# The xo projection and the MLP in one block, weights split by halves of K in a ring of five

## The reference, cut to what matters

```python
    o = jnp.einsum("bhsm,bmhd->bshd", probs, v).reshape(bsz, s, D_MODEL)
    return o @ w_xo                                   # 1024 x 1024, added to x
...
        x = x + memory_cross_attention(rms_norm(x, norm_xattn[i]), mem_n, w_q[i], w_kv[i], w_xo[i])
        hm = rms_norm(x, norm_mlp[i])                 # y = x * rsqrt(mean(x*x) + 1e-6) * gain
        x = x + jnp.square(jax.nn.relu(hm @ w_up[i])) @ w_down[i]     # 1024 -> 4096 -> 1024
    return rms_norm(x, norm_final)
```

## Time and profile before

| | us |
|---|---|
| median of 3 runs | 3066.21 (3064.24 to 3067.56) |
| span of the profiled execution | 3067.1 |
| PE busy in it | 2940.0 (96%) |
| DVE, POOL, ACT busy | 1510.3, 1127.4, 769.7 |
| mean granted clock of PE | 0.987 of full |

### The profile page before, as it was taken

One profiled execution on the slowest core, in us unless ns is written; L12 is line 12 of the kernel. 1 busy time (PEld: TensorE's weight loads), 2 busy tenths in 40 slices (PEclk: granted clock), 3 DMA queues, 4 the chain that ended last, 5 costly groups with the idle time before them and its releaser, 6 DMA issues. The chain is left out here.

```text
span 3067.1 us, 48431 instructions
## 1 busy us (share of the span) xinstructions
PE 2940.0 (96%) x20270; PEld 2330.9 (76%) x20270; DVE 1510.3 (49%) x1510; ACT 769.7 (25%) x1106; POOL 1127.4 (37%) x632
## 2 busy tenths in 40 slices
PE   7999888999999999999999999999999799989999
PEld 6776777778878767788888888777887677866677
DVE  6454443233375343741615235677678433357561
ACT  5433232320011032100100001324233332357410
POOL 1331223444344412444444444411221453435552
PEclk8999999999999999999999999999999999999999
DMA  6243332442141101111111111122233534321143
GB/s 213 75 134 114 96 93 78 139 121 69 40 139 55 55 28 42 48 48 42 50 45 48 48 48 48 42 62 83 84 102 95 164 106 126 114 86 63 57 139 124
DMA packets 324919, 258.05 MB, mean 84 GB/s; under 512 B 46754, under 2 KB 285529, under 8 KB 324746
## 3 DMA queue, kind: packets, MB, share of 16 engines
q1 hardware_dynamic: 324490, 255.47, 27.7%
q10 hardware_dynamic: 256, 0.07, 0.0%
HBM read 191.79 MB, written 63.31 MB: 83 GB/s over the span
## 5 line engine op out<-in xcount | busy, mean ns | idle before, releaser
L160 POOL TENSOR_TENSOR w_hi<-w_raw,ones 128x1024 fp32r<-128x1024 f32 x162 | 392.0, 2420 | 1080.5 <-PE ps L279 798.1
L279 PE MATMUL ps<-h_hi,w_hi 128*128 128x512 f32 x2096 | 670.1, 401 | 7.3 <-POOL w_lo L176 3.7
L279 PE MATMUL ps<-h_lo,w_hi 128*128 128x512 f32 x2096 | 647.4, 390 | 0.0
L279 PE MATMUL ps<-h_hi,w_lo 128*128 128x512 f32 x2096 | 646.6, 390 | 0.0
L279 PEld LDWEIGHTS ps<-h_hi,w_hi 128*128 128x128 f32 x2096 | 392.2, 188 | 119.1 <-issue 35.9
L279 PEld LDWEIGHTS ps<-h_lo,w_hi 128*128 128x128 f32 x2096 | 394.3, 188 | 83.8
L279 PEld LDWEIGHTS ps<-h_hi,w_lo 128*128 128x128 f32 x2096 | 394.0, 188 | 82.9
L163 POOL TENSOR_TENSOR w_lo<-w_raw,w_hi 128x1024 fp32r<-128x1024 f32 x162 | 426.4, 2632 | 12.7
L176 POOL TENSOR_TENSOR w_lo<-w_raw,w_hi 128x1024 fp32r<-128x1024 f32 x30 | 73.1, 2437 | 306.3 <-ACT w_hi L171 306.3
L736 ACT CAST hid_hi<-w_raw 128x512 f32 (+1 forms) x64 | 39.7, 622 | 574.2 <-DVE w_raw L764 574.2
L279 PE MATMUL ps<-branch_hi,w_hi 128*128 128x512 f32 x512 | 161.9, 397 | 6.5 <-POOL w_lo L163 2.0
(11 more groups left out here) (505 smaller groups left out, 4197.3 us busy)
## 6 DMA issues: line engine op xcount, KB each, us to landing
w_raw<-in_w_in_dram SPq DMA_DIRECT2D x91, 512.0 KB, 4.9
w_raw<-in_w_up_dram SPq DMA_DIRECT2D x32, 512.0 KB, 4.0
w_raw<-in_w_down_dram SPq DMA_DIRECT2D x32, 512.0 KB, 4.1
kv_raw<-in_w_kv_dram SPq DMA_DIRECT2D x16, 512.0 KB, 5.3
mix_gates<-mix_sig SPq DMA_DIRECT2D x16, 512.0 KB, 3.0
mix_gate_b<-mix_gates SPq DMA_DIRECT2D x32, 256.0 KB, 4.1
mix_gates<-w_raw SPq DMA_DIRECT2D x16, 512.0 KB, 2.8
x_in<-in_x_dram SPq DMA_DIRECT2D x8, 512.0 KB, 9.4
```

The costliest lines, as they stand in the source:

```text
L160: pool.tensor_tensor(c.w_hi[:, s], c.w_raw[:, s], c.ones[:].unsqueeze(1).broadcast_to([P, KT, P]), ALU.mult).then_inc(c.w_rounded, 1)
L279: last = pe.matmul(o, w[:, s, k], a[:, k - offset, (half + h) * width:(half + h + 1) * width], start=(k == kts[0] and w is c.w_hi and a is ...
```

## The change

1. `add_product` for xo and `mlp` become one block, `xo_mlp`. Nothing is rolled into loops any more.
2. The stationary operands are halves of K (4 k x 128 columns) in a ring of five slots over the space of `w_hi` and `w_lo`; `w_raw` is a ring of three loads. ACT rounds each half (`round`), POOL only subtracts (`rest`, half as long an instruction as before, and half as many elements in all, since it no longer rounds).
3. The MLP has eight groups of 512 hidden units: 4 up tiles, then 8 down operands that each hold all 4 k of an output tile. A down product is made half by half of the positions, 12 matmuls into one bank; banks 5, 6 and 7 go round. DVE adds each half to x apart.
4. The hidden units: DVE makes relu(p)·factor into SBUF (line 1004) and relu(p)·that back into the same PSUM bank (line 1007), so the factor stands there once, as 1/(mean + eps), with no root. ACT rounds from PSUM, DVE subtracts from PSUM. The bank is free for the next up tile only after this subtraction (`hid_ready`).
5. The norm's factor: PE sums the squares by columns (8 fp32 matmuls with 2 moving columns, line 818) behind up tile 0; DVE adds eps and takes the reciprocal of 128 x 16; PE spreads it again (8 fp32 matmuls of 128 columns, line 834) behind up tile 1, in two halves that both go through bank 7, ACT copying each to SBUF (`act_keep`).
6. The last group prepares the second block's input as before, but beside down products of half the length (24 matmuls for a tile instead of 48); accumulators and squares lie elsewhere in SBUF.
7. The DMA scratch of the program is set to 1024 bytes, which moves all of SBUF's tensors down by 15360 bytes.

```diff
-def mlp(c):
...
+    def round(self, act, o):
...
+        wait(act, self.used, o - RING + 1)
+        self.wait_loaded(act, unit)
+        act.copy(self.hi(o)[:], src).then_inc(self.rounded, 1)
...
+    def pe_spread(self, pe, h):
+        c = self.c
+        pe.wait_ge(self.inverted, 2)
+        wait(pe, self.kept, h)
+        for t in range(4):
+            one = self.columns[:, 2 * (4 * h + t):2 * (4 * h + t) + 1].broadcast_to([P, P])
+            last = pe.matmul(c.ps[:, self.bank, t * P:(t + 1) * P], one, c.ident[:], start=True, stop=True, skip_group_check=True)
+        last.then_inc(self.spread, 1)
...
+    def bank_of(g, n, place):
+        return 5 + (16 * g + 2 * n + place) % 3
...
+            def up(g, n):
+                m = HK * g + n
+                for u in range(2):
+                    wait(pe, hid_ready, 2 * m + u - 3)
...
+                if m == 0:
+                    norm.pe_columns(pe)
+                if m == 1:
+                    norm.pe_spread(pe, 0)
+                    norm.pe_spread(pe, 1)
...
+            def down(g, n):
+                o = s.down_op(g, n)
+                for place, h in enumerate(down_halves(n)):
+                    wait(pe, down_free, 16 * g + 2 * n + place - 2)
+                    last = s.product(pe, o, ps[:, bank_of(g, n, place)], lambda k: hid_hi[:, k, half[h]], lambda k: hid_lo[:, k, half[h]])
+                    last.then_inc(s.used if place else half_done, 1)
...
+                for n in range(KT):
+                    s.round(act, s.down_op(g, n) + 4)
+                    if g == GROUPS - 1:
+                        act.wait_ge(down_free, 16 * g + 2 * n + 2)
+                        late.act(act, n)
...
+            def evict(m, h):
...
+                v.mark(dve.scalar_tensor_tensor(out=r, in0=ps[:, bank], scalar=0.0, in1=norm.factor[:, half[h]], op0=ALU.max,
+                                                op1=ALU.mult))
+                v.wait(dve)
+                dve.scalar_tensor_tensor(out=ps[:, bank], in0=ps[:, bank], scalar=0.0, in1=r, op0=ALU.max,
+                                         op1=ALU.mult).then_inc(evicted, 1)
...
+            for g in range(GROUPS):
+                for n in range(HK):
+                    m = HK * g + n
+                    if m == 0:
+                        dve.wait_ge(norm.kept, 2)
+                    for h in range(2):
+                        evict(m, h)
+                    for h in range(2):
+                        split_hidden(m, h)
```

More of the change, by code:

```diff
@@ L19 @@
 LN_X_EPS = 64e-5
+TILES = SEQ // P
 _INS = [
@@ L358, in __init__ @@
         at_w = lambda slot, name: c.nc.alloc_sbuf_tensor_at(name, [P, SEQ], F32, offset=c.w_base + 4096 * slot)
-        self.sq.append(at_w(2, "late_sq")[:])
-        self.acc.append(at_w(5, "late_acc1")[:])
+        self.sq = [tail(c, 8192 + 4096 * n, f"late_sq{n}", [P, SEQ])[:] for n in range(2)]
+        self.acc = [tail(c, 4096 * n, f"late_acc{n}", [P, SEQ])[:] for n in range(2)]
         self.root = at_w(5, "late_root")
@@ L656, in _ @@
                     dve.tensor_tensor(self.out[t][:], self.out[t][:], c.ps[:, t], ALU.add).then_inc(self.taken, 1)
-def mlp(c):
[L661 to L765, removed]
-                            for h in range(2):
-                                dve.wait_ge(rounded, n + (h + 1))
-                                cut = slice(h * HALF, (h + 1) * HALF)
-                                dve.tensor_tensor(hid_lo[:, k, cut].rearrange("p a n -> p (a n)"), relu[:, h],
-                                                  hid_hi[:, k, cut].rearrange("p a n -> p (a n)").bitcast(F32),
-                                                  ALU.subtract).then_inc(ready, 1)
-                    def down_turn(i):
-                        for u in range(2):
-                            w_down.done(dve, i, u)
-                            if g:
-                                dve.wait_ge(down_free[u], (g - 1) * pairs + i + 1)
-                            rows = c.x[:, bass.ds(i * 2 + u, 1), :].rearrange("p a n -> p (a n)")
-                            dve.tensor_tensor(rows, rows, c.ps[:, 4 + 2 * u:6 + 2 * u, :].rearrange("p b n -> p (b n)"),
-                                              ALU.add).then_inc(down_free[u], 1)
-                    rolled(dve, pairs, up_turn)
-                    if g < groups - 1:
-                        rolled(dve, pairs, down_turn)
-                for k in range(KT):
-                    w_down = streams[-1][1]
-                    w_down.done(dve, k // 2, k % 2)
-                    dve.wait_ge(down_free[k % 2], (groups - 2) * pairs + k // 2 + 1)
-                    dve.tensor_tensor(c.x[:, k], c.x[:, k], c.ps[:, 4 + 2 * (k % 2):6 + 2 * (k % 2), :].rearrange("p b n -> p (b n)"),
-                                      ALU.add).then_inc(down_free[k % 2], 1)
-                    if k:
-                        late.dve_rest(dve, k - 1)
-                    if k > 1:
-                        late.dve_add(dve, k - 1)
-                late.dve_rest(dve, KT - 1)
-                late.dve_total(dve)
-    return streams[0][0], build
@@ L4554, in first_block @@
     query(late)
-    xo_weights = residual_weights(c, d["w_xo"][0])
-    attention(c, xo_weights)
-    up_weights, hidden = mlp(c)
-    late = LateNorm(c, "norm_mlp", up_weights, h, "norm_mlp")
-    add_product(c, "xo", xo_weights, branches, late)
+    stream = HalfStream(c)
+    attention(c, stream)
     final = LateNorms(c, second_weights(c), h)
-    hidden(late, final)
+    xo_mlp(c, stream, branches, final)
     return final
@@ L4578 @@
     arrays = {f"in_{name}_dram": np.ascontiguousarray(inputs[name]) for name in _INS}
[L4579 removed]
+    nc = bacc.Bacc("TRN2", target_bir_lowering=False, num_devices=1, dynamic_dma_scratch_size=1024)
     dram = {name: nc.dram_tensor(f"in_{name}_dram", list(arrays[f"in_{name}_dram"].shape), F32, kind="ExternalInput").ap()
```

263 lines of the change are left out of this document (261 added, 2 removed).

## The result

| | before | after |
|---|---|---|
| median of 6 runs each, side by side | 3067.89 us (3064.24 to 3070.30) | 3078.41 us (3073.65 to 3080.82) |
| ratio | | 1.0032, 95% interval 1.0021 to 1.0043 |
| span of the profiled execution | 3067.1 | 3075.6 |
| first xo matmul of tile 1 to first split matmul of the next stage | 808.36 | 817.63 |

The changed kernel is 0.32% slower, a difference of 10.5 us where 3078.41 and 3067.89 are compared and 8.5 us between the two profiled executions. The stage of the change alone is 9.27 us longer (1178.77 to 1996.40, against 1180.63 to 1988.99); everything outside it differs by 0.8 us.

What follows compares the result with a forecast made beforehand. PE, going from matmul to matmul without a gap, was taken to bound the stage. 3067.1 + 8.4 (norm's wait, clock, block end) + 0.6 (tail and end) = 3076.1 profiled, 3075.2 at the median, said as 3075; range 3067 to 3084.

Steps and rivals of the forecast that it cites:

- PE waits for the norm's factor at tile 2: Third up tile: PE waits for spreads, ACT's copies and DVE's subtraction of tile 0; +7.9 us, standing still about 0.9 and 5.1.
- half clock behind it: Clock at 0.50 after a wait: +1.2 us behind the norm's wait (bounds 0 and 3.4), +1.7 behind the last down product's.
- block end gone: Between xo and MLP: the old block's end disappears, -0.7 us.
- wait in the last down product: Operand 7, half 1, waits for its bank while DVE's addition is late in turns with POOL: +3.2 us, bounds 0 and 5.6.
- PE idle at the end: Before the next stage: PE starts 1.45 us after its own last matmul instead of 3.28, -1.8 us.
- clock at the end: Start of the next stage: a wait of 1.5 us keeps the clock up, -2.5 us.
- The tail: Last down operands to the next stage: POOL's four splits alternate with DVE's work; 3.2 + 1.7 - 1.8 - 2.5 = +0.6 us.
- U: The moment when down operand 5 of the last group is done; DVE's list was to end at U + 25.8 us.
- The rival of a covered tail: Rival A, last tiles: they keep PE's pace and only the norm's wait is left; +4.1 us, 3070; chance 0.18.
- the rival of higher costs: Rival B: full clock falls at both waits, the end's fall stays, 2 us at group ends; 3083 us; chance 0.12.
- The rival that was faster: Rival C: moved hidden units let 1536 down matmuls run at the up rate, -10.1 us; 3065 or 3060; 0.08 with D.
- D: Rival: the change does not do what it says, say tile 2 does not wait; -0.7 for 8.4, 3066 us; 0.08 with C.

Runs made afterwards that it cites:

- The experiment that removes it: The changed kernel with the norm's two spreads moved from behind up tile 1 into it (k = 1 and 3): 3067.69 us, 0.9999 of before.
- the base at 64 bytes: Auxiliary area aligned to 64 bytes (32 bytes up): in the kernel before 3067.13 us (0.9993), in the changed kernel 3076.13 us (1.0029).
- five banks: The changed kernel with five PSUM banks instead of three for the last group's down products: 3079.57 us, 1.0032 of before.
- ACT rounds: The changed kernel with ACT rounding the next block's first two weight tiles, leaving POOL two instructions instead of four: 3073.67 us, 1.0019 of before.
- small scratch: The kernel before with only the DMA scratch set to 1024 bytes: 3069.07 us, 1.0004 of before.
- same offset: The kernel before, DMA scratch at 1024, auxiliary area at the weights' offset modulo 512 bytes: 3051.35 us, 0.9934 of before.
- the last two runs: Auxiliary area at the weights' offset modulo 512: changed kernel with spreads inside tile 1 and ACT rounding 3045.43 us (0.9916); before with small scratch 3051.35 (0.9934).
- the three aligned runs: Auxiliary area aligned to 64 bytes in before (3067.13 us), in the changed kernel (3076.13), and in that with spreads inside tile 1 and ACT rounding (3064.78).
- both repairs: The changed kernel with the spreads inside up tile 1 and ACT rounding the next block's first two weight tiles: 3069.42 us, 1.0003 of before.

## Why the prediction was right

The forecast was 3075 us in a range of 3067 to 3084, and slower by more than 0.2% with 0.68; the median is 3078.4. Its terms against the trace:

| term | predicted | measured |
|---|---|---|
| PE waits for the norm's factor at tile 2 | +7.9 | +7.8 |
| half clock behind it | +1.2 | +2.1 |
| block end gone | -0.7 | in the remainder |
| column sums, xo, weights ring | 0 | 0 (1.70 us; 78.47 us; no wait) |
| wait in the last down product | +3.2 | +2.7 |
| half clock behind it | +1.7 | +1.7 |
| PE idle at the end | -1.8 | -1.3 |
| clock at the end | -2.5 | -2.9 (in these two executions) |
| stage | +9.0 | +9.27 |

The measured rows, with the -0.7 taken as predicted, add up to 9.4, of 9.27.

- **The first wait** has the length and the parts foretold: 0.77 idle for ACT's copy (predicted 0.9), 4.85 for DVE's subtraction (5.1). The experiment that removes it gives the time back. That a wait so short can be put down to order alone was the useful step: no engine was overloaded.
- **The clock behind it** is the term that was mis-sized. I took 1.2 between 0 and 3.4. The fall began at 1286.3, 2.3 us ahead of PE's return, and lasted 6.8 us, so that 4.4 lay on dense products: 2.1. What such a fall costs is in part chance. The same wait stands in three other kernels, and by the same reckoning, to the first pair at full pace, it cost 2.2 in after, 1.5 with the base at 64 bytes, 1.6 with five banks and 2.5 where ACT rounds. The rule of the Trainium skill, "TensorE: Matmul & The Clock Gate", section "Loop structure matters more than you think", that a nest which lets PE wait between products runs them cold, agrees with this trace at both new waits (0.50 for 6.8 and for 3.4 us); that it is no law for every wait shows at the end of the stage.
- **The tail** went by the turns between POOL and DVE. DVE's end came 25.4 us behind U (1964.83), predicted 25.8. That it is the work beside POOL, not the ring of banks, is shown by the five banks (same ratio) and by ACT's rounding (no wait left in the tail). The price in the median is small, since the gain is handed back at the end of the stage.
- **The clock at the end** came as foretold (-2.9 for -2.5), with some luck. That a wait of some 1.5 us keeps the clock up is borne out: the three kernels with 1.94 there stayed at 1.00. But before's fall, which the term takes as won, is not in every execution. In four profiled versions of the kernel before, PE waits the same 3.27 or 3.28 us, and the eight fp32 records then take 6.00, 4.80 (small scratch), 4.80 (same offset) and 3.10 us. The last is the one with the base at 64 bytes, whose end ran at 1.00:

```profile
1980.61 3.67 PE L3263 MATMUL ps<-late_acc,ones 128*128 128x512 f32 x8 [3.27 <-PEq L4509]
1983.71 1.02 PE L279 MATMUL ps<-h_hi,w_hi 128*128 128x512 f32 x2
```

  Against an execution like that one the change loses 11.15 us in the stage (816.11 and 804.96, both with the base at 64 bytes) and not 9.27. The tail, +0.2 in the sum above, is then some +3.
- **The rival of a covered tail** (3070) falls with the 2.50 us of idle time at 1975.88; **the rival of higher costs** (3083) with a clock that stayed at 1.00 at the end and with groups that end without a wait.
- **The rival that was faster** named the place of the moving operand as what parts 0.2267 from 0.2333. The change did not move that (109 down matmuls in 25 us, before and after), so as a forecast it was wrong. As a reading of the earlier trace rows it was right, and I gave its mechanism too little: the argument against it, that new places differ by multiples of 16384, spoke only against this change altering it, not against the effect. (D stands with the faster ones in the chances, though its 3066 would be no change that can be told; it was given almost nothing.)
- **The median** lies 3.4 us above the forecast. The base is 1.7 of them: the forecast starts from 3066.21, the median of three runs of the kernel before, which over six runs is 3067.89. The difference is the other part: 10.5 at the medians where 9.0 was forecast and 8.5 separate the two profiled executions. Those 2.0 us lie in which executions were profiled: a run's time is 1.7 above its core's span (3077.27 and 3075.6), so after's was 1.1 below its median and before's, with 3067.1, about 0.9 above its own.

## What to carry to other kernels

Where one engine is at its own rate through a stage, relief of the others buys nothing, and a new order mostly risks a wait: look for the instruction that makes that engine wait for something it has itself to start, and start it one tile earlier, inside running products. A wait that a longer ring of buffers removes comes back at the next meeting point if the consumer's total work is unchanged. When two stretches of the same instruction run at different rates, 3% apart, print the addresses of the operands before anything else: here that was worth about twice what the change cost (19.7 us at the medians in the kernel before).

## What the runs showed of the hardware

- **A matmul's pace depends on how the two operands lie to each other.** A 128 x 512 fp32r matmul with its own weight load starts every 0.2267 us where the stationary and the moving operand have the same offset modulo 512 bytes, and every 0.2333 on average where not. Seen: 128 and 128 (up, and down in the last two runs) 0.2267; 128 and 224 (xo, down) 0.2333; 128 and 256 (the three aligned runs) 0.2333. Why it is so no run shows. And not the value 128 but the equality counts: in the kernel before, the memory's keys multiply operands that both lie at 224, and PE's timeline has two starts in 0.45 us:

```profile
49.96 0.61 PE L2557 MATMUL ps<-kv_hi,mem_lo 128*128 128x512 f32 x2
50.41 0.62 PE L2557 MATMUL ps<-kv_lo,mem_hi 128*128 128x512 f32 x2
50.87 0.39 PE L2557 MATMUL ps<-kv_hi,mem_hi 128*128 128x512 f32 x1
```

  The weights' slices lie 512 bytes apart and all run alike, and distances of 96 and 128 bytes were both slow, so the period is 256 or 512; a distance of 256 was not tried, nor was it tried to move the weights instead.
- **The clock's fall behind a wait is not the same in every execution.** Behind idle times of PE of 4.85, 3.74, 2.96 and 2.50 us the clock was 0.50 for 3.4 to 6.8 us, behind 1.94 and 1.06 it was not. But one of 2.96 (both repairs, 1983.36) passed at 1.00, and so did the 3.27 of before with the base at 64 bytes, so length alone does not decide; the same 4.85 us cost between 1.5 and 2.5 us of dense work in four kernels. Small changes upstream thus shift a few us at the end of a stage, and a single profiled execution cannot tell edits of that size apart.
- **DVE and POOL in turns.** Over four POOL instructions in a row two DVE sums took 6.75 us instead of 2.35: each DVE instruction waits for a whole instruction of POOL. With two POOL instructions instead of four (ACT rounds) two sums beside one of them took 4.57, one such wait. The lock of whole instructions that the Trainium skill describes ("SBUF — State Buffer", section "Who interferes with whom") fits these numbers, and so does that DVE's additions, with an input in PSUM, took 1.27 for two beside POOL and without it; a shared bandwidth is harder to fit, since it would have stretched each instruction alike (argued, not tested).
